# Regrouping the last chunk's routing and the first expert's side work in a one-core MoE decoder step

## The reference, cut to what matters

```python
x1 = layer_norm(DN_ALPHA * x + mix, ln1_g, ln1_b)
logits = x1 @ w_router + b_router            # 32 experts
top_v, top_e = lax.top_k(logits, 4)
gates = jax.nn.softmax(top_v, axis=-1)
# every expert, on the tokens that chose it:
h = xb @ w1[e] + b1[e]                       # 1024 x 2048
a = glu * jax.nn.sigmoid(1.702 * glu) * (lin + 1)
out = a @ w2[e] + b2[e]                      # 1024 x 1024
x2 = layer_norm(DN_ALPHA * x1 + moe(x1), ln2_g, ln2_b)
y = x2 + jax.nn.sigmoid(x2 @ w_ple_gate) * (p @ w_ple)
```

## Time and profile before

| what | us |
|---|---|
| median of three runs (lowest, highest) | 1104.46 (1104.17, 1105.55) |
| the profiled execution | 1105.6 |
| its span, first to last instruction | 1103.8 |
| PE busy in the span | 1077.7 (98%) |
| DVE busy | 436.8 (40%) |
| ACT busy | 159.5 (14%) |
| POOL busy | 78.9 (7%) |
| memory read over the span | 436.61 MB, 399 GB/s mean |

### The profile page before, as it was taken

One profiled execution on the slowest core, in us unless ns is written; L12 is line 12 of the kernel. 1 busy time (PEld: TensorE's weight loads), 2 busy tenths in 40 slices (PEclk: granted clock), 3 DMA queues, 4 the chain that ended last, 5 costly groups with the idle time before them and its releaser, 6 DMA issues.

```text
span 1103.8 us, 14800 instructions
## 1 busy us (share of the span) xinstructions
PE 1077.7 (98%) x5616; PEld 425.9 (39%) x5616; DVE 436.8 (40%) x1109; ACT 159.5 (14%) x306; POOL 78.9 (7%) x107
## 2 busy tenths in 40 slices
PE   9999999999999999999999999999999999999998
PEld 7786433333333333333333333333333333333344
DVE  1648663333333333333333333333333333333345
ACT  1532341100000000000000000000000000000033
POOL 0747420000000000000000000000000000000000
PEclk9999999999999999999999999999999999999999
DMA  9989989999999999999999999999999999999961
GB/s 319 267 313 399 287 352 395 428 436 428 429 432 435 423 433 433 433 427 435 433 429 432 433 433 427 432 433 433 428 433 435 426 431 433 432 423 428 425 243 40
DMA packets 41027, 440.69 MB, mean 399 GB/s; under 512 B 8816, under 2 KB 16236, under 8 KB 25653
## 3 DMA queue, kind: packets, MB, share of 16 engines
q1 hardware_dynamic: 39945, 439.00, 95.4%
q0 software_dynamic: 368, 0.57, 0.2%
q10 hardware_dynamic: 676, 0.59, 0.2%
HBM read 436.61 MB, written 3.77 MB: 399 GB/s over the span
## 4 chain that ended last, share of the span: by engine, by line
PE 65%; DMA 20%; DVE 9%; issue 2%; POOL 2%; ACT 1%; DVEq 0%; SPq 0%; ACTq 0%; POOLq 0%
PE bank L1024 27%; DMA ring<-in_w_mlp 19%; PE bank L1104 16%; PE bank L971 4%; PE bank L605 3%; DVE proj L1663 3%; PE bank L1184 3%; PE bank L784 3%; DVE proj L1660 2%; DVE proj L1658 2%; PE bank L1085 1%; PE bank L984 1%; POOL ring L2141 1%; PE bank L1019 1%; PE bank L977 1%
## 5 line engine op out<-in xcount | busy, mean ns | idle before, releaser
L1024 PE MATMUL bank<-ring,proj 128*64 128x512 f32 x2024 | 461.5, 597 | 9.0 <-DMA ring<-in_w_mlp 9.0
L1624 DVE SCALAR_TENSOR_TENSOR xT<-bank,proj,xT 128x512 f32<-128x512 f32 x128 | 90.2, 746 | 428.3 <-PE bank L971 427.1
L1024 PEld LDWEIGHTS bank<-ring,proj 128*64 128x64 f32 x2024 | 137.6, 136 | 288.9 <-issue 263.0
L1104 PE MATMUL bank<-ring,pool_side 128*64 128x512 f32 x1024 | 226.8, 595 | 0.4 <-ACT pool_side L1993 0.4
L1104 PEld LDWEIGHTS bank<-ring,pool_side 128*64 128x64 f32 x1024 | 71.7, 137 | 133.3 <-issue 130.4
L1987 ACT ACTIVATE proj<-proj 128x256 f32<-128x256 f32 x64 | 26.7, 417 | 527.5 <-DVE proj L1657 527.5
L1615 DVE TENSOR_SCALAR proj<-bank,ln_rows_of_fours 128x64 f32<-128x64 f32 x256 | 67.4, 335 | 24.8 <-PE bank L984 24.8
L971 PE MATMUL bank<-mixT 64*128 64x512 f32 x264 | 74.5, 641 | 0.5 <-ACT mixT L1996 0.5
L605 PE MATMUL bank<-xT,ring 128*128 128x264 f32 x320 | 74.3, 388 | 0.3 <-ACT proj L1809 0.3
L605 PEld LDWEIGHTS bank<-xT,ring 128*128 128x128 f32 x320 | 59.9, 190 | 12.3 <-issue 1.6
L950 PE MATMUL bank<-xreg,proj 128*64 128x512 f32 x248 | 58.5, 592 | 0.0
(11 more groups left out here) (371 smaller groups left out, 634.6 us busy)
## 6 DMA issues: line engine op xcount, KB each, us to landing
ring<-in_w_mlp SPq DMA_DIRECT2D x77, 4096.0 KB, 27.6
ring<-in_w_mlp SPq DMA_DIRECT2D x36, 2048.0 KB, 14.9
ring<-in_w_in SPq DMA_DIRECT2D x9, 1024.0 KB, 14.9
ring<-in_w_out SPq DMA_DIRECT2D x4, 1024.0 KB, 8.8
ring<-in_w_ple_gate SPq DMA_DIRECT2D x4, 1024.0 KB, 26.9
xreg<-in_x_prompt SPq DMA_DIRECT2D x4, 512.0 KB, 4.1
ring<-q_row SPq DMA_DIRECT2D x1, 2048.0 KB, 7.0
ring<-k_row SPq DMA_DIRECT2D x1, 2048.0 KB, 7.3
```

The lines of the kernel that those rows point to most:

```text
L1024: last = pe.matmul(first_bank(t, q), xgT[:, k % 4, k // 4, :], first_columns(rows_, t, q), start=False, stop=(k == KD - 1))
L1104: last = pe.matmul(bank[4][BLOCK * h:BLOCK * (h + 1), :], aT[:, m, BLOCK * t:BLOCK * (t + 1)], w[:, k % 2, 512 * h:512 * h + 512], start=F ...
L1624: ins = STT(total[:, c, s], ins_bank[h][:, :], gate_table[:, c, bass.ds(n, 1)], total[:, c, s], ALU.mult, ALU.add)
```

## The change

1. `router(1, 6)` and `logit_rows(2)` are replaced. `router_early` does the four k of the first half while the second half is still being summed. `router_late` adds the other four with the turned rows as the stationary side and the router weights as moving columns, four copies side by side. It takes the early parts in through one matmul with `stack4`. Turning and routing alternate by quarters: turn quarter 0, k 4 and 5, turn quarter 1, k 6 and 7.
2. `route` makes the mask from the top 4 (padded to 8 with large numbers) by replacement and one comparison, instead of indices, cast, comparison and sum.
3. The diagonal of `before16` holds -FAR, so the count of places comes out masked and `place_rows` goes. Chunk 0's places are counted inside `mix`. Chunk 2's one-hot matrix is made on ACT by Abs and Relu. The shift of the norm of chunk 1 is made on POOL.
4. The gather for expert 0 is done in two parts of 256 columns in each half, each copied out by ACT by itself.
5. `early_embedding` of half 0 goes from ahead of the loop into expert 1, that of half 1 from expert 0 into expert 2, `early_samples` from expert 1 into expert 3. `spread_places(0)` goes from ahead of the loop into expert 0, after k = 2.
6. In expert 0 the combines come after k = 3, 5 and 6, and the wait on `comb_read` ahead of product 6.
7. `load_late(1)` leaves SP and is issued by ACT at the start of expert 3.
8. On DVE the starting work is put in another order: gate sums first, the starting sums behind them, `hot_turned` last. The memset of the samples' sum goes to POOL.

```diff
 # SP
                 load_next(n)
-                if n == SLOTS + 18:
-                    sp.wait_ge(sem("ple_ps"), 3)
-                    load_late(1)
...
 # PE, ahead of the loop
+            def router_early():
+                pe.wait_ge(sem("x1T_done"), 4)
+                for k in range(4):
+                    last = pe.matmul(logits_bank[1][32 * k:32 * k + EXPERTS, 0:P], wrout[:, k, :], x1T[:, k, P:2 * P],
+                                     start=True, stop=True)
+                last.then_inc(sem("part_ps"), 1)
+
+            def router_late(ks, done):
+                if ks[0] == 4:
+                    pe.wait_ge(sem("part_done"), 3)
+                    pe.matmul(LAST_LOGITS.rearrange("p (r e) -> p r e", r=4), LOGIT_PARTS[1],
+                              stack4.unsqueeze(1).to_broadcast([P, 4, EXPERTS]), start=True, stop=False)
+                pe.wait_ge(sem("x1T_done"), done)
+                for k in ks:
+                    last = pe.matmul(LAST_LOGITS.rearrange("p (r e) -> p r e", r=4), x1T[:, k, P:2 * P],
+                                     wrout[:, k, :].unsqueeze(1).to_broadcast([P, 4, EXPERTS]), start=False, stop=(k == KD - 1))
...
-            keep_dense(1)
-            turn_quarter(0)
-            turn_quarter(1)
-            pe.matmul(bank[3][:, 0:3 * EXPERTS], ones16[0:1, :], far_row, start=True, stop=False)
-            count_places(0, (1,))
-            count_places(2, (1,))
-            router(1, 6)
-            keep_dense(2)
-            logit_rows(2)
-            keep_dense(1)
-            pe.wait_ge(sem("ln1_ready"), 4)
-            pe.wait_ge(sem("onehot_ready"), 1)
-            gather_chunk(0)
-            gather_chunk(2)
-            pe.wait_ge(sem("mask_ready"), 3)
-            count_places(1, ()).then_inc(sem("pos_ps"), 1)
-            pe.wait_ge(sem("ple_in"), 16)
-            early_embedding(0, (0,))
+            turn_quarter(0)
+            router_late((4, 5), 5)
+            turn_quarter(1)
+            router_late((6, 7), 6)
+            pe.matmul(FIRST_PLACES[1], ones16[0:1, :], far_row[:, 0:EXPERTS], start=True, stop=False)
+            count_places(0)
+            count_places(2)
+            pe.wait_ge(sem("ln1_ready"), 4)
+            pe.wait_ge(sem("onehot_ready"), 2)
+            gather_part(0, 0)
+            gather_part(0, 1)
+            pe.wait_ge(sem("early_hot"), 3)
+            gather_part(2, 0)
+            gather_part(2, 1)
+            pe.wait_ge(sem("mask_ready"), 3)
+            count_places(1).then_inc(sem("pos_ps"), 1)
+            keep_dense(1)
...
-            gather_chunk(1).then_inc(sem("gathered"), 1)
-            turn_places()
-            pe.wait_ge(sem("xg_copied"), 1)
-            turn_gathered()
-            pe.wait_ge(sem("places_split"), 1)
-            pe.wait_ge(sem("onehot_ready"), 3)
-            spread_places(0)
-            early_embedding(0, (1,))
+            gather_part(1, 0).then_inc(sem("gathered"), 1)
+            pe.wait_ge(sem("ln1_ready"), 6)
+            gather_part(1, 1).then_inc(sem("gathered"), 1)
+            keep_dense(2)
+            pe.wait_ge(sem("xg_copied"), 2)
+            turn_gathered()
+            turn_places()
...
 # PE, in an expert; COMBINE_AT = ((1, 3, 5), (3, 5, 6))
+                first_one = opening and j == 0
-                    if k == 5:
+                    if k == COMBINE_AT[first_one][2]:
                         pe.wait_ge(sem("comb_read"), n * 3 + 3)
...
-                    if opening and j == 0 and k in (1, 3):
-                        early_embedding(1, (k // 2,))
-                    if opening and j == 0 and k == 1:
-                        pe.wait_ge(sem("ple_done"), 1)
-                    if k == 1:
+                    if opening and j == 0 and k == 2:
+                        pe.wait_ge(sem("places_split"), 1)
+                        spread_places(0)
+                    if opening and j in (1, 2) and k in (1, 3):
+                        early_embedding(j - 1, (k // 2,))
+                    if k == COMBINE_AT[first_one][0]:
                         combine(0, (j + 1) % 2)
-                    elif k == 3:
+                    elif k == COMBINE_AT[first_one][1]:
                         combine(1, (j + 1) % 2)
-                    elif k == 5:
+                    elif k == COMBINE_AT[first_one][2]:
                         combine(2, (j + 1) % 2)
-                        if opening and j == 1:
+                        if opening and j == 3:
                             early_samples()
...
 # DVE, route
-                step(dve.max_index(idx8[0:n, :], top[0:n, c, :], logits[0:n, c, :]))
-                step(dve.tensor_copy(idx4[0:n, :], idx8[0:n, 0:TOPK]))
-                step(TT(oh4[0:n], cst[0:n, C_EXP:C_EXP + EXPERTS].unsqueeze(1).to_broadcast([n, TOPK, EXPERTS]),
-                        idx4[0:n, :].unsqueeze(2).to_broadcast([n, TOPK, EXPERTS]), ALU.is_equal))
-                with nc.allow_low_precision(reason="a sum of zeros and at most one one"):
-                    step(dve.tensor_reduce(mask[0:n, c, :], oh4[0:n].rearrange("p k e -> p e k"), AX.X, ALU.add),
-                         "mask_ready")
+                step(dve.match_replace(others[0:n, :], top[0:n, c, :], padded[0:n, c, :], -PAD))
+                step(TS(mask[0:n, c, :], others[0:n, 0:EXPERTS], -PAD, None, ALU.is_equal), "mask_ready")
...
 # ACT
+            parts_out(2)
+            act.wait_ge(sem("pos_ps"), 2)
+            act.copy(pos_table[:, 0:3:2, 0:EXPERTS], bank[4][:, 256:256 + 2 * EXPERTS].rearrange("p (c e) -> p c e", c=2))\
+               .then_inc(sem("early_hot"), 1)
             turned_quarter(0)
             turned_quarter(1)
             ln1_root(2, 1)
-            parts_out(2)
+            act.activation(hot, cst[:, C_SLOT:C_SLOT + BLOCK], ACT.Abs, bias=pos_table[:, 2, 0:1], scale=-1.0)\
+               .then_inc(sem("early_hot"), 1)
+            act.activation(hot, hot, ACT.Relu, bias=ones[:, 0:1], scale=-1.0).then_inc(sem("early_hot"), 1)
...
-                if j == 0:
-                    embedded_early(1)
-                elif j == 1:
+                if j in (1, 2):
+                    embedded_early(j - 1)
+                elif j == 3:
                     act.wait_ge(sem("ple_ps"), 3)
                     act.copy(embedded_samples, EMBED_BANKS[2][0][:, 0:256]).then_inc(sem("ple_done"), 1)
+                    act.dma_start(late[1], unit_weights(EXPERTS - 2 * STEP, 1)).then_inc(sem("late_in"), 16)
                 expert(j, j)
```

More of the change, by code:

```diff
@@ L45 @@
 FAR = 16384.0
+PAD = 2.0 ** 127
+PADS = 8 - 4
 ALPHA = 2.0 ** 0.25
@@ L50 @@
 SLOTS = 16
+COMBINE_AT = ((1, 3, 5), (3, 5, 6))
 SLOT = 2048
@@ L872, in _ @@
             logit_rows(1)
+            pe.wait_ge(sem("mask_ready"), 1)
+            pe.matmul(FIRST_PLACES[0], ones16[0:1, :], far_row[:, 0:EXPERTS], start=True, stop=False)
+            pe.matmul(FIRST_PLACES[0], before16, mask[:, 0, :], start=False, stop=True).then_inc(sem("pos_ps"), 1)
             mix(1, second, range(6, KD), (1,))
@@ L894, in early_samples, with count_places @@
                 last.then_inc(sem("ple_ps"), 1)
-            def count_places(a, later):
+            def count_places(a):
                 m = CHUNKS[a][1]
-                if a == 1:
-                    pe.matmul(bank[3][:, EXPERTS:2 * EXPERTS], before16[0:m, :], mask[0:m, 1, :], start=False, stop=False)
-                for c in later:
-                    pe.matmul(bank[3][:, c * EXPERTS:(c + 1) * EXPERTS], ones16[0:m, :], mask[0:m, a, :],
-                              start=False, stop=False)
+                pe.matmul(FIRST_PLACES[1], (before16 if a == 1 else ones16)[0:m, :], mask[0:m, a, :], start=False, stop=False)
@@ L1543, in _ @@
             step(dve.memset(pos_table, FAR))
+            more(dve.memset(padded[:, :, EXPERTS:], PAD))
+            dve.tensor_copy(sel[:, 0, :], cst[0:3 * EXPERTS, C_SEL:C_SEL + 1].to_broadcast([3 * EXPERTS, P]))\
+               .then_inc(sem("onehot_ready"), 1)
             ln1_scale(0, 0)
@@ L1709, in _ @@
                          groups[1], ALU.mult, ALU.mult), "sample_begun")
-            for i in range(3):
-                gates_of(i)
-            begin_sum(total[:, 1, :], 1, "total_ready")
+            for c in range(2):
+                begin_sum(total[:, c, :], c, "total_ready")
+                further_places(c)
+            hot_turned(0, 0)
+            dve.wait_ge(sem("dve_chain"), counts["dve_chain"])
             dve.wait_ge(sem("passes_ready"), 1)
```

155 lines of the change are left out of this document (87 added, 68 removed).

## The result

The changed kernel takes 1111.31 us (median of 10 runs, 1109.21 to 1115.67), the kernel before 1105.13 in the 10 runs beside it. The ratio is 1.0057, with a 95% interval of 1.0048 to 1.0065. That is slower by more than the 0.2% that can be told apart; 1106.1 was forecast, and the range ended at 1108.0. The profiled execution took 1110.19 us, its span is 1108.4 against 1103.8 before. All ratios leave out two executions in a slow state: one of 1244.41 us (mean granted clock 0.851) of the kernel before with four idle matmuls, and one of 3648.07 us of the kernel before.

The account below looks back on a forecast made before the run. The saturated weight stream was taken as the bound: quad 48 issued 1.5 us later, minus 2.25 backlog, plus 2.42 for the spare unit, gives +1.65 us on the median of 1104.46, so 1106.1; range 1103.2 to 1108.0 (8 in 10).

Parts of the forecast that it names:

- The bound: Whole kernel: the saturated expert-weight stream sets the end; quad 48 waits for expert 2's end on PE.
- Part 1: Route to first product: gather starts 0.35 us earlier, first product at 147.2, 1.4 us earlier (bounds 146.7 and 148.2).
- The term of 0.4 for PE's register load: Just ahead of the first product: the register load, no longer covered by embedding, shows 0.4 us, from nothing to 1.29.
- Part 2: Experts 0 to 2 on PE: moved work and a stall add 2.9 us; with the earlier start, expert 2 ends 1.5 later.
- cover of 1 us: Combine 1 of expert 0: DVE's first sum ends near 158.4, PE needs it at 159.4; only lateness beyond 1 us counts.
- DVE's first sum comes too late: Combine 1 of expert 0 waits for the reordered DVE chain; 2.5 us late gives 1107.6; chance 0.17 shared with register load.
- the stall: Expert 0, behind combine 1: PE waits once for DVE's two sums ahead of product 6, 1.56 us.
- the faster rival: Experts 1 and 2 have room for the embedding, so expert 2 ends 2.7 us earlier: 1102.0; chance 0.1.
- Its variant in which only the stall is missing: Expert 0: only the 1.56 us PE wait behind combine 1 is absent: 1104.5; chance 0.1, shared with a better start.
- Part 3: Weight stream from quad 48 on: its backlog is gone, the spare unit comes behind it; later landings move by +1.65 us.
- the formula: From quad 48 on: issue lateness minus 2.25 us backlog plus 2.42 for the spare unit; 1.5 - 2.25 + 2.42 = +1.65.
- the cover of 2.25: Stream at quad 48's issue in the kernel before: a backlog of 2.25 us, worked out from landings.

Follow-up runs that it names:

- the first two runs: Kernel before with two idle matmuls added in expert 1, then with four in experts 1 and 2: 1105.95 and 1108.63 us, against 1104.95.
- POOL later: Changed kernel with POOL's split of the sample rows made to wait until DVE has done `hot_turned(0)`: 1108.24 us (ratio 1.0038).
- changed kernel, repeat: Changed kernel with no edit, run again later on the same chip as the repeated run with two idle matmuls around combine 1: 1109.98 us (1.0054).
- no waits, four idle matmuls: Changed kernel with POOL's split delayed, expert 0's combine 2 behind product 7, and four idle matmuls ahead of the gather: 1110.54 us (1.0057).
- fillers, second time: Changed kernel with one idle matmul ahead of and one behind combine 1 of expert 0, repeated beside the unchanged one: 1109.72 us (1.0044).
- fillers, first time: Changed kernel with one idle matmul ahead of and one behind combine 1 of expert 0: 1110.37 us (1.0041).
- no waits: Changed kernel with POOL's split behind `hot_turned(0)` and expert 0's combine 2 moved behind product 7, its `comb_read` wait directly ahead: 1109.60 us (1.0043).
- the run without the unit's load: Changed kernel without the load of the spare unit `late[1]`, its product using what lies in the tile: 1110.79 us (1.0058).

## Why the prediction was wrong, point by point

**The bound was right.** The stream, saturated from slice 8 or 9 on, sets the end. Quad 48 and the end of expert 2 are the point, as the idle stream at 238 to 240 us and the first two runs show.

**Part 1: right in kind, 0.6 short (0.2 without the offset).** The gathers start at 142.02 and 144.73, where 140.85 and 143.5 were worked out; they stood at 141.21 and 144.33 before. PE's two router pieces, at 139.58 and 140.97, each wait for ACT's copy (0.24 and 0.46 us), so a quarter costs 1.39 us in this alternation, and PE comes to the gather later than before instead of 0.35 earlier. Some 0.36 of that is this execution's own offset (99.92 against 99.56). From chunk 1's gather to the first product PE takes 3.03 us, against 4.25 before (148.58 - 144.33) and 3.7 in the working. The term of 0.4 for PE's register load cost nothing (from the bias matmuls at 147.30 to the product are 0.46 us, as before). The step that failed here is the start of the gather, chunk 1's by 1.23 us; the first product is 0.8 earlier instead of 1.4. The gather in halves cost nothing: 2.09 us against 2.08. ACT's Abs and Relu took 0.34 and 0.35 us with no table load between them and the square root, as the page "ScalarE: Activation LUTs" of the Trainium skill has it (Table sets: the hidden batching unit).

**Part 2: the failed step.** It said that DVE's chain "ends near 158.4" with a "cover of 1 us". The first sum ended at 161.03, and PE paid 1.28 us. The term that was put at nothing is what POOL's subtraction does to DVE's chain: it made a step 1.68 us longer (1.97 for 0.29), and the run with POOL later puts the whole 1.28 on it. Without it the sum ends at 159.69, which is still 1.3 later than worked out, and combine 1 starts at 160.07, so 0.4 us of the cover of 1 was left. That is not the length of DVE's own chain: from the scaling to the end of the sum it takes 12.2 us there (147.47 to 159.69), and 12.45 were worked out (145.95 to 158.4). It began late, at 147.14 instead of 145.95 in the changed kernel, since the scaling follows the gather of part 1. PE made up for the late gather in its 3.03 us and DVE's chain did not, which took 0.6 of the cover. The rival "DVE's first sum comes too late" named this wait and a time of 1107.6, but blamed the reordering and, together with the register load, got 0.17. The rule of "SBUF — State Buffer" of the Trainium skill (Who interferes with whom) was in my hands, and I asked only what it does to POOL. It holds for both sides: the one that comes second stands until the other is done. DVE's step came second, and it was the one on the path. The trace agrees (1.97 us instead of 0.29, ending 0.16 after POOL's). What I had asked of it did not happen: POOL's three gate tables took 2.61 us, against 3.32 before, and its last sample part ended at 161.32 and not near 164.

The rest of part 2 holds. From the first product to the end of expert 2 PE takes 91.25 us (239.01 - 147.76) against 86.87 before (235.45 - 148.58), +4.38. The sum said +2.9, and the unforeseen wait of 1.28 with the 0.16 by which the stall was longer (1.72 for 1.56) makes +4.34. The embedding cost its full price in experts 1 and 2 (the end of expert 0 is 0.31 later than before, that of expert 2 3.56), so the faster rival is out. Its variant in which only the stall is missing was not had by order alone: it came back ahead of the transposes, 2.38 us for 0.33.

**Part 3: the formula was right, its input wrong.** With +3.56 in place of +1.5 the working gives 3.56 - 2.25 + 2.42 = +3.7. Measured are +1.6 at quad 48 (the formula: +1.3) and +4.4 at the landing at 314.5 (310.1 before), +4.6 in the span. In the other profiled executions with the spare unit behind the quad the formula comes out within 0.2 us (all against the kernel before):

| run | quad 48 issued later by | formula | span longer by |
|---|---|---|---|
| POOL later | 2.6 | 2.8 | 2.7 |
| changed kernel, repeat | 3.0 | 3.2 | 3.1 |
| no waits, four idle matmuls | 3.2 | 3.4 | 3.3 |
| fillers, second time | 3.6 | 3.8 | 3.9 |
| fillers, first time | 4.5 | 4.7 | 4.8 |
| no waits | 4.6 | 4.8 | 4.7 |
| changed kernel | 3.6 | 3.7 | 4.6 |

So the last row is the odd one: its quad took 12.4 us where the others took 12.0 to 12.2 (12.15 worked out), another 0.25, and the remaining 0.6 us lies in the landings behind it and stays open. So does a miss of 0.7 in the run without the unit's load, where the formula gives 3.3 - 2.25 = +1.0 and the span is +1.7. In the runs of the table the quad lands 2.0 to 2.4 us less late than it is issued, which is the cover of 2.25; in the first two it was 1.3, with the pair ahead of the quad not yet landed.

**A term that was missing: the clock.** "The clock is no term here" was read from a kernel in which PE has no such waits. With waits of 1.28 and 1.72 us in expert 0, 8 of 15 executions show a lowered clock and take about 2 us more, and that lifts the median. The whole excess over the forecast's +1.65 is 6.2 - 1.65 = 4.5 us: 1.28 for POOL, 0.16 for the longer stall, 0.24 for the start without the offset, about 1.6 between the median of all (1111.31) and that of the executions at a clock of 1.0 (1109.68), and 1.2 that stays open. Of this 1.2 the profiled execution shows 0.36 as its own offset, 0.25 as the lone quad and 0.6 in the landings, but the repeat shows none of the three. That the clock falls after such a wait is shown once, in the run with 2.38 us. In the two profiled executions of the changed kernel the mean is 1.0: the first has PE busy for 2.20 of 5 us from 160 to 165, and the granted clock stays at 1.00 up to 182. That it falls at these two waits in the executions of lower clock is thus inferred, from the 16 of 32 against 2 of 131.

## What to carry to other kernels

Before a step is moved on GpSimd, list the VectorE instructions with two SBUF operands that will stand beside it, and ask which side is on the path; here VectorE's step, which was, got 1.7 us longer beside an instruction of 1.98 us. A queue's backlog at the one point where a load waits for compute is the whole budget of a change ahead of it: work it out from two landings, spend it once, and count the load that you move behind that point in full. Waits of TensorE that are worth 1 to 2 us in a sum went here with a lowered clock and some 2 us more in half of the executions, so fill them with work that is due anyway rather than taking work out of them.

## What the runs showed of the hardware that I had not expected

- A DVE `tensor_tensor` of 128x128 with both operands in SBUF took 1.97 us instead of 0.29 beside POOL's of 8x1024, which itself took 2.61 instead of 1.98 (when it began at 155.56, another DVE instruction with two SBUF operands was running, from 155.11 for 1.22 us). DVE's sum with a PSUM operand kept its 1.41 beside the same POOL instruction.
- The granted clock fell to 0.50 after a PE wait of 2.38 us. PE had been busy for 5.00 of 5 us in each of the two stretches up to 165 us and for 2.67 of 5 in the one with the wait; the clock was at 1.00 again from 176 us on. In the changed kernel PE was busy for 2.20 of 5 us and the clock stayed at 1.00.
- Of 32 executions of kernels with a PE wait of 1.7 us or more in expert 0, 16 had a mean granted clock of 0.998 or less, of 131 without one, 2.
- The mean granted clock tells such executions apart by only 0.002 to 0.004.
- A load of 4.2 MB into an empty queue lands after 12.0 to 12.4 us (eight profiled executions), and 9.7 us after the one ahead of it when the queue is full: 2.3 to 2.7 us for an empty queue, as 2.4 us for a load of 2.1 MB.
- Two profiled executions of the same kernel reached the same matmul 0.6 us apart (99.31 and 99.92), so positions are best compared from a common instruction.
